# A hybrid attention and HGRN2 decoder step: keys and values accumulated during the modulation, w_ada products inside dense tiles, token norm by accumulated squares

## What is computed

```python
mod = silu(c) @ w_ada + b_ada              # 6 vectors of 1024 for each of 9 sequences
sh_a, sc_a, g_a, sh_m, sc_m, g_m = split(mod, 6)
h = rms_norm(x, norm_mix) * (1 + sc_a) + sh_a
z = h @ w_in                               # k, v, q, and the inputs of HGRN2 and of the gates
o_attn = sink_attention(q, k, v, ...)      # sliding window, sinks, ALiBi
o_rec  = hgrn2_chunked(...)
x = x + g_a * ((sigmoid(ga) * o_attn + sigmoid(gr) * o_rec) @ w_out)
h2 = rms_norm(x, norm_mlp) * (1 + sc_m) + sh_m
x = x + g_m * (square(relu(h2 @ w_up)) @ w_down)
y = rms_norm(x, final_norm)
```

## Time and profile before

| | |
|---|---|
| Median of 3 runs | 1237.44 us (1236.23 to 1239.28) |
| The profiled execution's own time | 1236.89 us |
| Its span, first to last instruction | 1235.1 us |
| Mean granted clock of TensorE | 0.969 |
| Instructions | 22212 |
| Read from HBM, written | 109.2 MB, 11.8 MB |

### The profile page before, as it was taken

The page is one execution under the profiler, slowest core; times in us unless marked ns, Lnnn a source line. Parts: engine busy times, 40 slices in busy tenths (PEclk is TensorE's granted clock), DMA queues, the critical chain, the costliest instruction groups (busy, mean ns, idle before and its releaser), DMA issues.

```text
span 1235.1 us, 22212 instructions
## 1 busy us (share of the span) xinstructions
PE 1146.0 (93%) x8917; PEld 1084.5 (88%) x8917; DVE 711.1 (58%) x1449; ACT 538.5 (44%) x950; POOL 182.3 (15%) x144
## 2 busy tenths in 40 slices
PE   5789999988999989999998999789999999999996
PEld 4688788966998978989988999589999999999996
DVE  5726554455487666476686655554463644636464
ACT  3433556456536555655535323453232232232334
POOL 1400000000133223213032001141011010110100
PEclk9889999999999988999998999799999999999997
DMA  9683322222322312222222155212323222222202
GB/s 313 199 315 103 103 69 93 80 73 77 136 84 71 105 42 64 71 67 73 71 69 71 62 192 185 69 35 69 103 69 103 69 76 96 70 102 70 92 12 77
DMA packets 108778, 120.46 MB, mean 98 GB/s; under 512 B 2692, under 2 KB 98652, under 8 KB 108389
## 3 DMA queue, kind: packets, MB, share of 16 engines
q1 hardware_dynamic: 108677, 119.06, 29.4%
HBM read 109.22 MB, written 11.80 MB: 98 GB/s over the span
## 4 chain that ended last, share of the span: by engine, by line
PE 47%; DVE 7%; ACT 2%; issue 1%; DMA 1%; POOL 0%; DVEq 0%; ACTq 0%; POOLq 0%
PE PS L763 41%; DVE wR L1288 1%; PE PS L877 1%; PE PS L722 1%; DMA xT<-residual 1%; DVE xhat L1256 1%; PE PS L923 1%; DVE qt L1441 0%; DVE tmp L1272 0%; PE PS L680 0%; DVE kt L1442 0%; DVE att L1459 0%; PE PS L930 0%; DVE tmp L1271 0%; PE PS L920 0%
## 5 line engine op out<-in xcount | busy, mean ns | idle before, releaser
L763 PE MATMUL PS<-hR,wR 128*128 128x288 f32 x3744 | 533.4, 300 | 12.8 <-ACT tmp L1069 6.7
L763 PEld LDWEIGHTS PS<-hR,wR 128*128 128x128 f32 x3744 | 509.5, 191 | 23.3 <-ACT tmp L1069 7.7
L763 PE MATMUL PS<-actR,wR 128*128 128x288 f32 x1920 | 258.8, 295 | 2.0 <-DVE actR L1425 1.8
L763 PEld LDWEIGHTS PS<-actR,wR 128*128 128x128 f32 x1920 | 255.4, 188 | 3.4 <-DVE actR L1425 2.0
L1288 DVE TENSOR_TENSOR wR<-raw,wR 128x512 fp32r<-128x512 f32 x256 | 205.0, 801 | 71.5 <-ACT wR L990 64.1
L990 ACT ACTIVATE wR<-raw 128x512 fp32r<-128x512 f32 x256 | 161.9, 632 | 140.6 <-PE PS L763 132.9
L1588 POOL TENSOR_TENSOR D<-b 128x512 f32<-128x512 f32 (+1 forms) x56 | 68.2, 1217 | 508.2 <-PE PS L850 267.9
L1615 POOL TENSOR_TENSOR actR<-tmp,actR 128x576 fp32r<-128x576 f32 x32 | 46.2, 1445 | 304.8 <-DVE actR L1341 304.8
L1341 DVE CAST actR<-tmp 128x576 fp32r<-128x576 f32 x32 | 15.2, 476 | 129.5 <-ACT tmp L1088 129.5
L722 PE MATMUL PS<-wR,hR 128*128 128x256 f32 x600 | 82.8, 296 | 2.0 <-ACT kT L1056 0.9
L722 PEld LDWEIGHTS PS<-wR,hR 128*128 128x128 f32 x600 | 77.5, 200 | 5.1 <-issue 1.7
(11 more groups left out here) (212 smaller groups left out, 1214.7 us busy)
## 6 DMA issues: line engine op xcount, KB each, us to landing
raw<-in_w_in SPq DMA_DIRECT2D x30, 1024.0 KB, 5.1
raw<-in_w_up SPq DMA_DIRECT2D x16, 1024.0 KB, 5.3
raw<-in_w_down SPq DMA_DIRECT2D x16, 1024.0 KB, 4.9
mid<-in_w_ada SPq DMA_DIRECT2D x12, 1024.0 KB, 5.1
ada<-in_w_ada SPq DMA_DIRECT2D x8, 1024.0 KB, 13.3
S<-in_state_hgrn SPq DMA_DIRECT2D x8, 512.0 KB, 4.5
out_hgrn_sample<-S SPq DMA_DIRECT2D x8, 512.0 KB, 5.2
raw<-in_w_out SPq DMA_DIRECT2D x4, 1024.0 KB, 4.9
```

What stands on the lines that cost most here:

```text
L763: mm = pe.matmul(PS[:, 2 * x.pair + h, 0:HALF], weights(x, w, k, col), rhs[r], start=(k == 0 and n == 0), stop=(k == last and n == 2))
```

## The change

It has four parts.

1. **Opening.** The norm's factor is taken by token: ACT squares the untransposed input with an accumulator (one row sum per token), takes ln and exp of these columns (`rbt`), DVE scales five identity blocks by them (`diagonal`, kept in `tmp` and `tmp_s`), TensorE multiplies ones by these into banks 4 and 5, and ACT copies the result to `rb`. POOL's adds and the statistics of this norm go. `modulate` goes by single tiles. The order is written out anew: keys and values (both joint now, the value tiles two to a bank in banks 4 to 6) are accumulated in chunks of two k between the w_ada products, whose results stand in bank 7. The hi of keys and values is ACT's. The values' weights are loaded behind the fourth w_ada unit, not behind the eighth; the remaining lb operations on DVE move into `masks`.
2. **w_ada 8 to 19** stand by twos behind q0 to q3, rf0 and rq0. Each is a guest of a dense tile: product behind chunk 1, sum and mods behind chunk 2, in the other bank pair. Dense tiles alternate by a count `turn` of their own, and `FREED` gives for each tile the last one before it in its pair.
3. **Up units 0 and 1** are both joint: four tiles, in all four pairs, accumulated together. Modulation of tiles 0 and 1 is moved ahead, behind the mods of unit 21.
4. The split of the unit behind a joint group is done in one go (`split_ahead`) between its chunks.

The diff, cut to its core (the event orders, the bank assignment and the new norm; "..." marks what is left out):

```diff
     for u in w_in:
         out.append(u)
-        if rest:
-            out.append(rest.pop(0))
+        if u[0] == "q" or u in (("rf", 0), ("rq", 0)):
+            out += [rest.pop(0), rest.pop(0)]
...
-JOINT = (("k", 0), ("up", 0))
+JOINT = (("k", 0), ("v", 0), ("up", 0), ("up", 1))
...
-        self.pair = t % 2 + (2 if u < FRONT else 0)
...
+        if kind in ("q", "rf", "rq") and UNITS[u + 1][0] == "ada":
+            mine = [(u + 1, 0), mine[0], (u + 2, 0), mine[1]]
+            u += 2
...
+        if u in MID:
+            out.append(Tile(len(out), u, kind, i, n, None, (turn + 1) % 2))
+        elif kind == "v" or u < FRONT or (kind, i) == ("up", 1):
+            out.append(Tile(len(out), u, kind, i, n, None if kind == "ada" else splits.index(u), 2 + n if kind == "up" else None))
+        else:
+            out.append(Tile(len(out), u, kind, i, n, None if kind == "ada" else splits.index(u), turn % 2))
+            turn += 1
...
+    a = TILES[:FRONT]
+    yield from product(a[0])
+    yield ("hi", 0)
+    yield ("norm",)
+    yield from product(a[1])
+    yield from sums(0)
+    yield ("modulate", 0, 0)
+    yield from product(a[2])
+    yield ("modulate", 0, 1)
+    yield from product(a[3])
+    yield ("lo", 0, 0)
+    yield ("load", AFTER[SPLITS[0]])
+    yield from sums(1)
+    yield ("modulate", 0, 2)
+    yield from chunk(keys, 0)
+    yield from product(a[4])
+    yield ("modulate", 0, 3)
+    yield ("hi", 1)
+    yield from chunk(keys, 1)
+    yield from product(a[5])
+    yield ("lo", 1, 0)
+    yield ("load", AFTER[SPLITS[1]])
+    yield from sums(2)
+    yield ("modulate", 0, 4)
+    yield from chunk(values, 0)
+    yield from product(a[6])
+    yield ("modulate", 0, 5)
+    yield from product(a[7])
+    yield from sums(3)
+    yield ("modulate", 0, 6)
+    yield ("modulate", 0, 7)
+    yield ("load_mid", MID[0])
+    yield ("caches",)
+    yield ("tables",)
+    yield from chunk(values, 1)
+    yield from chunk(keys, 2)
+    yield from chunk(values, 2)
+    yield from chunk(keys, 3)
+    yield from split_ahead(2)
+    yield from chunk(values, 3)
...
+        if x is ups[0]:
             yield ("ada_sum", pending)
             yield ("evac", pending)
             pending = None
-        if x.kind == "up" and x.i == 0 and x.n == 0:
-            for k in range(0, KT, 2):
+            for k in range(2, KT):
                 yield ("modulate", 1, k)
+            for c in range(4):
+                for y in ups:
+                    yield ("mm", y, c)
+            yield from split_ahead(ups[-1].split + 1)
...
+            if guest and c == 1:
+                yield ("mm", guest, 0)
+                yield ("ada_part", guest)
+            if guest and c == 2:
+                yield ("ada_sum", guest)
+                yield ("evac", guest)
+                if guest.u != MID[-1]:
+                    yield ("load_mid", MID[MID.index(guest.u) + 1])
...
+                if x.kind == "ada" and x.i == 22:
+                    yield ("modulate", 1, 0)
+                    yield ("modulate", 1, 1)
...
-                    if u == 1:
-                        load(RING[0])
-                load(RING[1])
+                    if u in (1, 3):
+                        load(RING[u // 2])
...
+            def norm():
+
+                pe.wait_ge(s_diag, TT + 1)
                 pe.wait_ge(s_xe, KT + 1)
+                for i in range(TT + 1):
+                    rows = P if i < TT else SMP
+                    mm = pe.matmul(PS[:, 4 + i // TT, i % TT * P:i % TT * P + rows], ones[0:rows, :], diagonal(i), start=True, stop=True)
+                mm.then_inc(s_stat, 1)
...
+                if n < 2:
+                    act.wait_ge(s_raw[SLOT[u]], raw_loads(u))
+                    done(act.activation(wR[split_index(n)][:, 0, :], raw[SLOT[u]][:], ACT.Copy), s_hi, 4)
+                    return
...
+                act.wait_ge(s_x, (TT + 1) * 16)
+                for i in range(TT + 1):
+                    rows = P if i < TT else SMP
+                    done(act.activation(squared[0:rows, :], xn[0:rows, i, :], ACT.Square, accum_out=rbt[0:rows, i:i + 1]))
+                token_rms(None)
...
+                for i in range(TT + 1):
+                    dve.wait_ge(s_rbt, 1 if i < TT else 2)
+                    rows = P if i < TT else SMP
+                    done(dve.tensor_scalar(diagonal(i), ident[0:rows, 0:rows], rbt[0:rows, i:i + 1], None, ALU.mult), s_diag)
```

More of the change, by code:

```diff
@@ L234, in walk, with split_ahead, product, sums @@
     yield ("front",)
-    k_tile = TILES[first["k", 0]]
-    pairs = FRONT // 2
-    for p in range(pairs):
-        for x in TILES[2 * p:2 * p + 2]:
-            yield ("mm", x, 0)
-            yield ("ada_part", x)
-        if p == 0:
-            yield ("hi", 0)
-            yield ("lo", 0, 0)
+    keys, values = ([x for x in TILES if x.kind == kind] for kind in ("k", "v"))
+    ups = [x for x in TILES if x.kind == "up" and x.i < 2]
+    def split_ahead(n):
+        yield ("hi", n)
+        for q in range(4):
+            yield ("lo", n, q)
+        yield ("load", AFTER[SPLITS[n]])
+    def product(x):
+        yield ("mm", x, 0)
+        yield ("ada_part", x)
+    def sums(p):
         for x in TILES[2 * p:2 * p + 2]:
@@ L1241, in ada_part @@
                 dve.wait_ge(s_mm, x.t + 1)
[L1242 removed]
+                done(dve.tensor_copy(part[n % 2][:], ada_of(x)), s_part)
             def scale_vectors(n, k0):
@@ L1617, in _ @@
             for ev, *x in walk():
-                if ev == "norm":
-                    for k in range(KT):
-                        squares(0, k)
-                elif ev == "stats":
+                if ev == "stats":
                     squares(*x)
```

263 lines of the change are left out of this document (134 added, 129 removed).

## The result

The changed kernel is slightly slower: median 1243.46 us (1238.95 to 1252.29) against 1238.99 (1235.16 to 1242.89) of the kernel before on the same chips, ratio 1.005 [1.0032, 1.0067]. The forecast was 1210, faster.

What follows compares the result with a forecast made beforehand. TensorE, busy 93% of the span, was taken as the bound, other engines counting only where it waits or is slowed. Opening 10, attention stretch 12 and second norm 5 made 27 off 1236.9, forecast 1210 us, range 1198 to 1226.

Steps and rivals of the forecast that it cites:

- The opening, forecast 10: Start of the kernel to q: q's first dense matmul near 73 instead of 85.5, 10 us gained, bounds 3 and 15.
- The rival that the opening stays chained: Opening: the chain still ties TensorE, so it gives only 1 to 3 us; 1218 us, chance 17%.
- the walk through the new order: Opening: new instruction order timed with old durations; last modulated tile 59.6, remaining matmuls done at 73.
- the slower rival: Attention stretch: w_ada sums at chunk 2 wait for DVE, 4.2 us each, 50 in all; 1256 us, chance 7%.
- The attention stretch, forecast 12: 84 to 329 us: idle time and slow matmuls removed, less a new wait; 12 us gained, between 2 and 16.4.
- Gone: the 12.0 us of idle time: Attention stretch: dense matmuls' 12.0 us idle behind ACT read-outs disappears, as a tile's read-out has another tile to hide in.
- The five waits of scores on DVE stay: Attention stretch: the five waits of scores on DVE were to remain as before.
- The slow matmuls were to go: Attention stretch: slow matmuls after idle waits, counted at three places, disappear; 4.4 us gained.
- the new wait of 4.4: Attention stretch: TensorE waits for DVE's copy before the w_ada sum at chunk 2, 0.37 us a unit, 4.4 for twelve.
- the stretch gives it back: Attention stretch rival: score waits grow, so it gains only 2 us; 1220 us, chance 13%.
- The second norm, forecast 5: 778 to 817 us: earlier modulation lets 192 joint up matmuls run without wait; 5 us gained, between 2 and 8.
- The stretch from 330 to 778 should only be shifted.: Between attention stretch and second norm: only a shift in time was expected.

Runs made afterwards that it cites:

- the second profile: The changed kernel run again unedited, for a second profile: median 1247.16 us, ratio 1.0078 to the kernel before; the profiled execution took 1237.81.
- open2: open_up with the opening's queues reordered (low part of keys earlier, modulations ahead of part copies, fifth and eighth products ahead of chunks): 1219.96 us, ratio 0.9852.
- open_up: The changed kernel without guests, the middle w_ada units again tiles of their own behind twelve units: 1230.13 us, ratio 0.9939 to the kernel before.
- open2_cut: open2 with the twelve middle w_ada products cut from 256 to 8 columns: 1220.79 us, ratio 0.9863 to the kernel before.
- guests_cut: The changed kernel with open2's opening, its twelve guest products cut from 256 to 8 columns: 1229.93 us, ratio 0.9926 (uncut 1234.42, 0.9967).
- guests_late: The changed kernel with each guest's product and sum one chunk later in its dense tile: 1240.34 us, ratio 1.0025 to the kernel before.
- guests_rf: The changed kernel with guests in q0, q1 and both pairs' rf and rq units: 1239.19 us, ratio 1.0009 to the kernel before.
- lo_first: open_up with one line moved, VectorE taking the low part of the key weights right behind the norm's diagonals: 1229.44 us.

## Why the prediction was wrong

**The opening, forecast 10.** The rms vector came at 27.2 (27) and the first tile earlier, both right. The rival that the opening stays chained came true: q at 80.7, not 73; the last modulated tile at 68.4 (GpSimd's last two start at 65.46 and take 2.99), not 59.6. What was left behind the last sums took 18.0 us (62.76 to 80.74) for the 18.2 of the sum, so the error lies wholly ahead of that. The step that failed is the walk through the new order. I gave the first key chunk 3.2 us, though I had the row of 5.30 at half clock; it took 5.70. And I let each engine's work start when its input was there, without asking what was queued in front of it: a part copy that waits for a product behind a key chunk holds a modulation that needs nothing from it. That is the question which the slower rival asked of the attention stretch, and which I did not ask of the opening. My lower bound of 3 named the low clock; what was measured lies under it, 2.1 us by my own account (85.5 - 80.7 - 2.6, and 2.8 in the second profile) and 0.1 at the same clock against the old opening with the same units ahead of q. The two accounts differ in the price of the two w_ada units ahead of q: I put them at 2.6 us, and in the old opening q starts 4.7 earlier without them (85.47 to 80.81), part of which is clock (0.83 and 0.88). open2, 10 us faster than open_up, shows that the 10 us were there, for another order.

**The attention stretch, forecast 12.** The step that failed is "Gone: the 12.0 us of idle time". The wait was named by its releaser (a read-out by ScalarE) and I read it as the price of two tiles sharing banks. It was the lateness of ScalarE and VectorE. With the banks out of the way TensorE ran on to the next instruction that needed them, a score, and waited there: 12.0 and 6.2 became 0.0, 14.5, 4.5 and 2.3. "The five waits of scores on DVE stay" was wrong for the same reason. The slow matmuls were to go (4.4 us); instead the stretch's clock went from 0.98 to 0.95 and the other matmuls took 4.5 us more. No term had that, and why guests come with a lower clock stays open. In the sum's own terms: idle time +3.9 for -12.0, slow matmuls +4.5 for -4.4, the units that fell into the stretch less the ri chunk that fell out +2.7 (booked in the opening), and the new wait of 4.4 is within the idle time: +11.1 for -12. That a product costs its time was a silent assumption, too: in open2_cut and guests_cut some three fifths and half of what was cut came back as waits. The sum's wait was sized well (0.37 a unit forecast, 0.2 measured), and so the slower rival's mechanism did not occur; that the product itself would wait, 4.5 us in all, had no term. The result ended on its side all the same, by a mechanism that I had as a rival only with a gain: that the stretch gives it back.

**The second norm, forecast 5:** 5.2 in the changed kernel, 5.0 alone. The term and its mechanism were right: the joint matmuls ran without a wait. That the chain there had nothing else for TensorE to wait for is my reading of it; no run tests that.

**"The stretch from 330 to 778 should only be shifted."** In work, yes; in time it took 448.8 and 438.5 in two executions. No term has room for that. It was chance that the first profile had the longer one: its span is 11.5 us above that of the kernel before, the span of the second only 0.7 (1235.8).

What would have shown it beforehand: in the earlier trace rows not only the dense tile was late behind a w_ada product but VectorE's copy too, by 2.8 and 5.8 us. Two engines' queues stood behind ScalarE at the same places, and I took that for an effect of the place.

## What to carry to other kernels

A wait that names a late engine may not go away when the instruction that waits is freed: here it moved to the next one that needed the engine, in the changed kernel and again in guests_late. Small independent work is worth most just where such waits are (guests_rf), so before it is moved out of there, cut it to nothing in place and see what the waits and the time do, with the granted clock read beside them: here the clock hid or made up some 2.5 us of the answer. In a hand-written order, read each queue for what stands **behind** an instruction that waits: open2 is 10 us below open_up with six moved lines and not one operation less. This version, the change's opening in another order, its joint up units, and the w_ada units left as tiles of their own, is the fastest of all measured here (1219.96, ratio 0.9852 [0.9831, 0.9874]).

## What the runs showed of the hardware

**VectorE and GpSimd.** A VectorE operation of 64 columns took 1.37 us beside a GpSimd operation; one of the same size three operations earlier took 0.23. open_up, VectorE and then GpSimd:

```profile
32.86 0.23 DVE L1368 TENSOR_TENSOR tmp<-tmp,mods 128x64 f32<-128x64 f32 x1
33.12 0.76 DVE L1353 TENSOR_TENSOR xhat<-xT,rb 128x576 f32<-128x576 f32 x1
33.91 0.42 DVE L1339 COPY part<-PS 128x256 f32<-128x256 f32 x1
34.37 1.37 DVE L1367 TENSOR_TENSOR tmp<-xhat,mods 128x64 f32<-128x64 f32 x1
```

```profile
34.26 1.41 POOL L1665 TENSOR_TENSOR hR<-tmp,hR 128x576 fp32r<-128x576 f32 x1 [33.82 <-ACT hR L1135]
```

It ends at 35.74, just behind GpSimd's 35.67: it stood for all of the other's instruction that was left. The rule of the Trainium skill which I cited ("SBUF — State Buffer", "SBUF: two separate sides"), that the loser blocks for the whole instruction, agrees with these rows. It also agrees with the row that I held against it: when the lo began at 59.18, GpSimd's operation (58.15 and 2.20 long) had 1.17 us left, and the lo lost 1.03 (3.32 for 2.29). It did not matter much: in lo_first the low part of the keys no longer runs beside GpSimd, and that and its earlier place brought q forward by 0.6 us.

**The clock.** The untouched stretch, some 3,100 matmuls (one w_ada unit more in the programs that have the new opening and no guests), took 438.1 to 448.8 us in fourteen profiles of thirteen programs, with its granted clock between 0.98 and 0.95; a difference of a few us in one profile is no evidence for an edit. Why the attention stretch has a lower clock with guests, why the programs with guests vary more from run to run, and why the guests cost 6 us on the old opening and 13 to 17 on the new one, stays open: no run varied the clock alone.
